# Interleaving the first two up projections of each FFN in a two-layer transformer block kernel

## The reference

```python
def pre_norm(z, gain, mod, k):
    return rms_norm(z, gain) * (1 + mod[:, 3 * k + 1]) + mod[:, 3 * k]

def swiglu(x, w_in, w_out):
    a, b = jnp.split(x @ w_in, 2, axis=-1)
    return (jax.nn.silu(a) * b) @ w_out
...
    mod_l = (silu_c @ ada_w[i] + ada_b[i]).reshape(b, N_MOD, 1, d)
    h = h + 0.5 * mod_l[:, 2] * swiglu(pre_norm(h, norm_g[i, 0], mod_l, 0), ffn_w_in[i, 0], ffn_w_out[i, 0])
```

## Time and profile before

| | |
|---|---|
| median of 3 runs | 3390.02 us (3389.61 to 3390.06) |
| profiled execution, its own time | 3392.71 us |
| its span (first to last instruction) | 3391.0 us |
| granted TensorE clock, mean | 0.974 of full |
| VectorE busy | 1875.9 us (55%) |
| ScalarE busy | 852.9 us (25%) |
| weight units loaded | 183 of 1024 KB, 4.8 us each |
| modulation units loaded | 72 of 1024 KB, 5.0 us each |

### The profile page before, as it was taken

One profiled execution on the slowest core, in us unless ns is written; L12 is line 12 of the kernel. 1 busy time (PEld: TensorE's weight loads), 2 busy tenths in 40 slices (PEclk: granted clock), 3 DMA queues, 4 the chain that ended last, 5 costly groups with the idle time before them and its releaser, 6 DMA issues.

```text
span 3391.0 us, 41921 instructions
## 1 busy us (share of the span) xinstructions
PE 3094.6 (91%) x17076; PEld 2642.0 (78%) x17076; DVE 1875.9 (55%) x2689; ACT 852.9 (25%) x1109; POOL 41.0 (1%) x81
## 2 busy tenths in 40 slices
PE   0899999978999979999998999999899999979999
PEld 0788888866777768888887888888678787758887
DVE  6755465645555556465567545545644536464444
ACT  2211111234433431111123111112322313232221
POOL 0000000000000000000000000000000000000000
PEclk9999999988999989999998999999899999989999
DMA  6332232111010123232232322221111111112222
GB/s 226 131 118 99 88 115 106 62 44 38 30 44 27 47 75 137 87 111 101 97 111 78 108 88 87 74 74 62 62 38 62 62 49 62 49 62 87 99 87 86
DMA packets 39016, 277.33 MB, mean 82 GB/s; under 512 B 4337, under 2 KB 4593, under 8 KB 5937
## 3 DMA queue, kind: packets, MB, share of 16 engines
q1 hardware_dynamic: 27936, 197.45, 16.5%
q0 software_dynamic: 11024, 79.11, 6.6%
HBM read 274.44 MB, written 2.10 MB: 82 GB/s over the span
## 4 chain that ended last, share of the span: by engine, by line
PE 84%; DVE 10%; issue 3%; ACT 3%; DMA 1%; DVEq 0%; POOL 0%; POOLq 0%; ACTq 0%
PE ps L277 27%; PE ps L279 26%; PE ps L278 26%; PE ps L305 2%; PE ps L458 1%; DVE act_buf L1024 1%; DVE xnl L1030 1%; DVE ada_prod L972 1%; DVE adaw L972 1%; DVE wl L959 1%; DVE h L1042 1%; ACT wh L668 1%; DVE ssum L1005 1%; DMA adaw<-ada 0%; DMA c_act<-c_rows 0%
## 5 line engine op out<-in xcount | busy, mean ns | idle before, releaser
L277 PE MATMUL ps<-xnh,wl 128*128 128x512 f32 (+1 forms) x3008 | 1056.8, 351 | 63.3 <-DVE h L1042 31.4
L278 PE MATMUL ps<-xnl,wh 128*128 128x512 f32 (+1 forms) x3008 | 1048.8, 349 | 0.0
L279 PE MATMUL ps<-xnh,wh 128*128 128x512 f32 (+1 forms) x3008 | 1046.8, 348 | 0.0
L277 PEld LDWEIGHTS ps<-xnh,wl 128*128 128x128 f32 x3008 | 574.4, 191 | 154.5 <-issue 64.1
L279 PEld LDWEIGHTS ps<-xnh,wh 128*128 128x128 f32 x3008 | 574.0, 191 | 72.6
L278 PEld LDWEIGHTS ps<-xnl,wh 128*128 128x128 f32 x3008 | 574.6, 191 | 71.2 <-issue 1.0
L1042 DVE SCALAR_TENSOR_TENSOR h<-ps,coef,h 128x512 f32<-128x512 f32 x744 | 441.4, 639 | 182.3 <-PE ps L279 180.1
L668 ACT ACTIVATE wh<-raw 128x2048 fp32r<-128x2048 f32 (+1 forms) x183 | 342.3, 1871 | 619.1 <-PE ps L279 619.1
L959 DVE TENSOR_TENSOR wl<-raw,wh 128x2048 fp32r<-128x2048 f32 (+1 forms) x183 | 410.2, 2241 | 107.5 <-ACT wh L668 107.5
L277 PE MATMUL ps<-hidh,wl 128*128 128x512 f32 x1232 | 430.9, 350 | 20.7 <-DVE wl L959 10.3
L279 PE MATMUL ps<-hidh,wh 128*128 128x512 f32 x1232 | 427.4, 347 | 0.0
(11 more groups left out here) (207 smaller groups left out, 2938.6 us busy)
## 6 DMA issues: line engine op xcount, KB each, us to landing
raw<-weights SPq DMA_DIRECT2D x183, 1024.0 KB, 4.8
adaw<-ada POOLq DMA_DIRECT2D x72, 1024.0 KB, 5.0
h<-x_in SPq DMA_DIRECT2D x1, 3072.0 KB, 14.5
c_act<-c_rows POOLq DMA_DIRECT2D x2, 1024.0 KB, 10.0
out<-h SPq DMA_DIRECT2D x8, 256.0 KB, 2.0
cs<-rope_mla POOLq DMA_DIRECT2D x1, 512.0 KB, 3.5
cr<-rope_ret POOLq DMA_DIRECT2D x1, 512.0 KB, 3.9
dist<-dist_in POOLq DMA_DIRECT2D x1, 448.0 KB, 4.5
```

The lines of the kernel that those rows point to most:

```text
L277: mm(dst, lhs[1][rows], rhs[0][rows], start=first, stop=False)
L278: mm(dst, lhs[0][rows], rhs[1][rows], start=False, stop=False)
L279: return mm(dst, lhs[0][rows], rhs[0][rows], start=False, stop=last)
```

## The change

The first two up projections are no longer done one after the other. A new function `first_ups` waits for both slots, then takes the 8 row blocks of the latents in turn, and for each does all four groups: both halves of unit s0 into banks 1 and 0 and both halves of unit s1 into banks 4 and 3. Then the context groups of s0 follow, with `glu_full` behind them, and those of s1, with `glu_full` behind them. In the FFN without context both signals come together, behind the last row block. The programs of the other engines are as before, and so are the matmuls in number and size. The file is 10 lines longer, so lines of it behind L360 move by 10.

```diff
--- before.py
+++ after.py
@@ -316,20 +316,31 @@
             def ffn(n_streams, slot):
                 streams = STREAMS[:n_streams]
 
-                def up(j, s, first=False, wait_hid=True, y_left=0):
+                def first_ups(s0, s1):
+
+                    for s in (s0, s1):
+                        pe.wait_ge(w_ready[s], c.next(w_ready[s]))
+                    for k in range(KD):
+                        pe.wait_ge(xn_ready, c.next(xn_ready))
+                        for half, s, bank in ((1, s0, 1), (0, s0, 0), (1, s1, 4), (0, s1, 3)):
+                            ins = three(ps[:, bank, 0:S], w(s, k * 256 + half * P), xn(k, 0, S), k == 0, k == KD - 1)
+                    if n_streams == 1:
+                        ins.then_inc(glu_full, 2)
+                        return
+                    for j, s in enumerate((s0, s1)):
+                        for half in range(2):
+                            for k in range(KD):
+                                ins = three(ps[:, 3 * j + 2, L * half:L * half + L], w(s, k * 256 + half * P), xn(k, S, L),
+                                            k == 0, k == KD - 1)
+                        ins.then_inc(glu_full, 1)
+
+                def up(j, s, wait_hid=True, y_left=0):
 
                     pe.wait_ge(w_ready[s], c.next(w_ready[s]))
                     if wait_hid:
                         pe.wait_ge(hid_done, c.next(hid_done))
                     groups = [(1, 3 * j + 1, 0, STREAMS[0]), (0, 3 * j, 0, STREAMS[0])] + \
                         [(0, 3 * j + 2, 0, STREAMS[1]), (1, 3 * j + 2, L, STREAMS[1])] * (n_streams - 1)
-                    if first:
-                        for k in range(KD):
-                            pe.wait_ge(xn_ready, c.next(xn_ready))
-                            for half, bank, col, (t0, n) in groups[:2]:
-                                ins = three(ps[:, bank, col:col + n], w(s, k * 256 + half * P), xn(k, t0, n),
-                                            k == 0, k == KD - 1)
-                        groups = groups[2:]
                     for g, (half, bank, col, (t0, n)) in enumerate(groups):
                         if g == 1 and y_left:
                             pe.wait_ge(y_added, c.next(y_added, y_left))
@@ -354,8 +365,7 @@
                         ins.then_inc(y_full, 1)
 
                 s0, s1 = slot, 1 - slot
-                up(0, s0, first=True, wait_hid=False)
-                up(1, s1, wait_hid=False)
+                first_ups(s0, s1)
 
                 per = {w_ready[0]: 3, w_ready[1]: 3, hid_done: 4, y_added: 16, hid_ready: 4}
                 with c.loop(pe, BLOCKS // 2, per):
```

## The result

| | before | after |
|---|---|---|
| median, us | 3390.02 (5 runs, 3387.92 to 3390.45) | 3405.94 (5 runs, 3405.13 to 3406.84) |
| span of the profiled execution | 3391.0 | 3403.5 |
| its own time | 3392.71 | 3405.13 |

The change makes the kernel slower by 0.48%, ratio 1.0048 with a 95% interval of 1.0033 to 1.0063, some 16 us in the medians. The forecast was 3407.5.

A forecast was written before the change was run, and what follows sets the result against it. TensorE's stream was taken as the bound, with VectorE deciding in a few places. FFNs one to four, +8.2 - 1.2 + 4.2 + 6.3 = +17.5 us on 3390.0, gave 3407.5 us, range 3400 to 3414.

The forecast's parts named there:

- Second FFN, -1.2: Second FFN: loop starts at the end of the first answer's chain, 1.3 us earlier; -1.2 us taken.
- rival 3: Clock falls at every new wait, the 1.3 us ones ahead of the loop included: +5.7 us, 3413.2; chance 8%.
- First FFN, +8.2: First FFN: VectorE's queue of modulation units moves with the first glu_full, 8.2 us late, and TensorE waits for it.
- the first stretch at nothing: Start of each FFN: the new code's first matmuls run at the same lower clock as before, costing nothing.
- Third FFN, +4.2: Third FFN: TensorE waits 4.2 us for the product at m=2, +2.6 us, plus 1.6 for the lower clock behind.
- The allowance of 0.9 for a wait at m=3: Third FFN, if the clock stays high: piece m=3 waits for y_added of m=0, 0.9 us, giving +3.5.
- Fourth FFN, +6.3: Fourth FFN: both signals come last, TensorE idles 6.4 us, loop starts 4.2 us later, plus 2.1 for the lower clock.
- The clock's share: Fourth FFN: after idling, TensorE restarts at the lower clock, costing 2.1 us.
- The first (only waits go, 3379.5): All FFNs: the answers have cover enough, only the small waits go, gaining 10.5 us, 3379.5; chance 3%.
- the second (no queue): Refill of s0 is late but VectorE's idle times absorb the modulation queue's delay: +2.2 us, 3392.2; chance 4%.
- the fourth: Matmuls alternating between four groups run slower than 0.230 us, at 0.24: +3.4 us, 3410.9; 84% together with the forecast.
- The fifth (a denser start raises the clock sooner, 3398.3): Start of each FFN: no first matmuls at 1.2 GHz, 2.3 us better each, 9.2 in all, 3398.3; chance 1%.

The follow-up runs named there:

- e1: The kernel before with the new order in the fourth FFN alone, the old one in the other three: 3393.60 us, ratio 1.0013 to the kernel before.
- e6: The changed kernel plus 24 matmuls nobody reads behind the first two units in the fourth FFN, filling TensorE's idle time: 3405.01 us, ratio 1.0045 to the kernel before.
- e4: The changed kernel with the third FFN's modulation pair behind the first answer cut to 32 of 1024 columns, for timing alone: 3403.69 us, ratio 1.0045 to the kernel before.
- e3: The changed kernel with both glu_full signals of the first two units behind the last context group, TensorE's stream unchanged: 3425.99 us, ratio 1.0110 to the kernel before.
- e2: The kernel before with the new order in the first FFN alone: 3398.02 us, ratio 1.0028 to the kernel before.
- e7: The kernel before with s0's context groups going through the row blocks with its latents in the first three FFNs: 3379.95 us, ratio 0.9975 to the kernel before.

## Why the prediction was right

**The time.** 3407.5 was forecast and 3405.94 measured, +17.5 and +15.9 us; the range of 3400 to 3414 lay wholly above the kernel before. The two profiled executions differ by 12.5 us only. The kernel before stood 2.7 us above its median in its own; its first FFN took 1.5 us more there than in e1, and its attention and retention took 0.4 and 1.0 more than after, which is about that. So the path and the waits were right in every FFN, and the sizes of the terms missed by -1.0, +0.1, +0.7 and -1.4 us, which in part cancel.

**Second FFN, -1.2.** -1.1 in the profile, with a wait of 1.35 us for `wl` ahead of the loop. The small waits are gone and half of the gain is spent on the refill of s0. The clock did not fall behind this wait: 0.49 us is the duration of a first matmul at the higher clock, and the 48 latents' matmuls behind it take 11.0 us. It is the same at the two other waits of 1.35 us, so rival 3 is out.

**First FFN, +8.2.** +5.7 against the profile before, +7.2 against e1. The mechanism is as said: no idle time ahead of the second answer, waits of 9.36, 6.66 and 4.90 us. The term was too large by 1.0 us. The first stretch at the lower clock had 8 matmuls instead of 11, so the latents ended 23.5 us after the first row block instead of the 24.4 forecast, and `glu_full` was late by 7.3 us, from 21.9 to 29.2. The rest of the way down to +5.7 is the scatter shown above, a wait of 0.91 us for a modulation load where it had been 2.01 and the stretch in the middle of the loop before, less 1.2 us by which the half clock behind piece m=2 lasted longer (15.5 us from there to the down's end against 14.35; it is 15.6 in e1). I had set the first stretch at nothing, as TensorE didn't wait there. But the old order hid its length: whatever it was, the norm's pace caught up with it. The new order is paced by TensorE, and in it each matmul more at the lower clock delays the signal. In e6, which has the changed kernel's program in the first FFN, the stretch had 14 matmuls, and the latents ended 24.7 us after the first row block instead of 23.5. That is 1.3 us of the 2.9 by which the FFN is longer there (612.6 to 609.6). The rest is VectorE's wait for a modulation load, 2.70 us instead of 0.91:

```profile
158.61 1.23 DVE L984 CUSTOM_DVE_ANT_0 ada_prod<-adaw,c_act 128x1024 f32<-128x1024 f32 x1 [2.70 <-DMA adaw<-ada]
```

**Third FFN, +4.2.** +4.9, with the loop 1.14 us earlier and a wait of 4.19 for a wait of 4.2 forecast. The lower clock set in behind it, though not with its first matmul, and took the 1.6 us that the sum has for it. (The rows that the prediction cites for that term give 1.9; 1.6 is what the piece from 177.45 to 181.21 cost before, 3.76 us instead of 2.12.) The 0.7 that is missing lies in the product: 0.35 us because its chain started later, the latents having 12 matmuls at the lower clock and not 10, and 0.35 because VectorE's queue took 43.35 us from the start of `wl` (1850.37) to the fourth product (1893.72) instead of 43.0. e4 takes the wait away by shortening the queue alone. The allowance of 0.9 for a wait at m=3 wasn't needed; no such wait shows after.

**Fourth FFN, +6.3.** +4.9. The wait is 6.27 us for 6.4, and the clock behind it is half. The miss is again the first stretch: 14 matmuls at the lower clock were taken over from the rows of before, and there were 8, so that the first matmul at the higher clock came 3.5 us after the first row block instead of 6.1. Six matmuls at 0.43 instead of 0.23 are 1.2 us, and the loop started 2.8 us later than before instead of 4.2. The clock's share was given as 2.1; e6 measures 1.6.

**The rivals.** The first (only waits go, 3379.5) is refuted by e1 to e3, the second (no queue) by e2, the fourth by a pace of 0.227: 88 matmuls in 19.96 us, from 86.87 to 106.83. The fifth (a denser start raises the clock sooner, 3398.3) is out as well: the first matmuls at the lower clock are still there, 8, 12, 12 and 8 in the four FFNs, against 11, 12, 10 and 14 before, and in the first FFN of e6 the new order has 14. The chances given to the theories one by one, with the 2% for unseen cases, come to 102%, a slip; those of the three outcomes come to 100.

## What to carry over

When an engine waits in small steps, filling the steps is only half of the question; the other half is which signal the filling pushes back, and who has work of another kind queued behind that signal. The gaps filled with the next unit's matmuls, which delays the first unit's signal, lost 16 us; filled with the rest of the first unit's own, which brings the signal forward, they gained 8. A wait in a profile is no price tag: one of 9.4 us could be removed for nothing, since a queue further on set the end.

## What I had not expected of the hardware

The stretch at the lower clock at the start of a burst varies in length between executions and places: 6 to 14 matmuls in the first FFN, 14 in the fourth FFN of before and of e2, 6 to 9 there in all others, e7 with the old order among them. What sets it stays open. Single stretches of some eight matmuls at 1.2 GHz also occur in the middle of a loop, behind a wait of 1.8 us that passes without one in most turns. This is the kernel before, in the turn that starts at 346.73, and then the changed kernel 1.6 us behind the same wait:

```profile
348.30:351.40 3.10, 3.10 (x9) 2.42 (x8) 0.88 (x1) 0.00 (x0) 0.00 (x0) 0.50 0.28 66
```

```profile
355.10:358.20 3.10, 3.10 (x15) 2.57 (x14) 0.94 (x1) 0.00 (x0) 0.00 (x0) 1.00 0.27 53
```

Each costs 1.6 us. They come and go from one kernel to the next in the sections that were not changed, and limit what a section's length in a single profile can tell to about 2 us. In the first FFN VectorE's longest wait for a load of a modulation unit adds to that: 0.91 to 2.70 us among the ten profiles, 2.01 and 0.95 with the same old order (before and e1), 0.91 and 2.70 with the same new one (after and e6).
